# Squares folded in pairs, a root activation at a block's start, one block merged into two others, and an output stored in quarters

## The reference

```python
for l in range(2):
    sh1, sc1, g1, sh2, sc2, g2 = ada_params(c, ada_w[l], ada_b[l])       # and the same of c_ctx for ctx
    x = x + g1 * rmsnorm_2(mixer(modulate(x, norm_g[l, 0], sh1, sc1)), norm_g[l, 1])
    x = x + g2 * rmsnorm_2(swiglu(modulate(x, norm_g[l, 2], sh2, sc2)), norm_g[l, 3])
# rmsnorm_2(x, g) = x * rsqrt(mean(x * x) + 1e-6) * g;  modulate = rmsnorm_2(x, g) * (1 + scale) + shift
# the context rows go the same way in layer 0, and serve layer 1 as keys and values only
return x
```

## Time and profile before

| | us |
|---|---|
| median of 3 runs | 3593.79 (3592.45 to 3594.01) |
| the profiled execution | 3587.6 |
| its span | 3585.9 |
| PE busy | 3289.4 (92%) |
| DVE, ACT, POOL busy | 2146.1, 1456.4, 41.7 |
| granted TensorE clock, mean | 0.947 of full speed |

### The profile page before, as it was taken

One profiled execution on the slowest core, in us unless ns is written; L12 is line 12 of the kernel. 1 busy time (PEld: TensorE's weight loads), 2 busy tenths in 40 slices (PEclk: granted clock), 3 DMA queues, 4 the chain that ended last, 5 costly groups with the idle time before them and its releaser, 6 DMA issues. The chain is left out here.

```text
span 3585.9 us, 54305 instructions
## 1 busy us (share of the span) xinstructions
PE 3289.4 (92%) x20646; PEld 2841.2 (79%) x20646; DVE 2146.1 (60%) x4081; ACT 1456.4 (41%) x2274; POOL 41.7 (1%) x66
## 2 busy tenths in 40 slices
PE   6987899999999898999999999699889999979897
PEld 4844799998888677999997888488656787867797
DVE  4523489875777735699776788523673433244553
ACT  3312444444555434444444555323333332233443
POOL 0000000000000000000000000000120000000000
PEclk8988999999999999999999999799997999979999
DMA  5575576556888644676657787432453332321453
GB/s 186 157 237 191 183 219 202 173 177 186 242 242 242 197 130 153 195 206 183 176 176 222 242 242 241 133 96 65 166 193 96 102 99 88 94 61 52 123 166 123
DMA packets 225065, 596.61 MB, mean 166 GB/s; under 512 B 27424, under 2 KB 97440, under 8 KB 224576
## 3 DMA queue, kind: packets, MB, share of 16 engines
q1 hardware_dynamic: 220656, 588.17, 53.8%
q10 hardware_dynamic: 4176, 5.29, 0.5%
HBM read 558.16 MB, written 35.19 MB: 165 GB/s over the span
## 5 line engine op out<-in xcount | busy, mean ns | idle before, releaser
L2528 PE MATMUL ps<-h_split,split_layer 128*128 128x256 f32 x6144 | 773.1, 285 | 10.9 <-DVE split_layer L2317 10.9
L2528 PEld LDWEIGHTS ps<-h_split,split_layer 128*128 128x128 f32 x6144 | 746.5, 192 | 14.2 <-DVE split_layer L2317 14.2
L2674 PE MATMUL ps<-split_layer,h_split 128*128 128x512 f32 x3072 | 702.1, 391 | 13.9 <-DVE h_split L2658 13.9
L2674 PEld LDWEIGHTS ps<-split_layer,h_split 128*128 128x128 f32 x3072 | 580.4, 189 | 135.2 <-DVE split_layer L2641 14.3
L800 PE MATMUL ps<-h_parts_ffn,split_ffn 128*128 128x512 f32 (+1 forms) x2112 | 380.6, 341 | 21.2 <-DVE h_parts_ffn L273 12.0
L800 PEld LDWEIGHTS ps<-h_parts_ffn,split_ffn 128*128 128x128 f32 x2112 | 329.6, 191 | 73.7 <-issue 23.1
L2317 DVE TENSOR_TENSOR split_layer<-ring,split_layer 128x1024 fp32r<-128x1024 f32 x256 | 311.6, 1219 | 79.6 <-ACT split_layer L2456 78.0
L742 DVE TENSOR_TENSOR split_ffn<-ring,split_ffn 128x1024 fp32r<-128x1024 f32 x132 | 161.1, 1225 | 255.9 <-ACT split_ffn L724 247.1
L2641 DVE TENSOR_TENSOR split_layer<-ring,split_layer 128x1024 fp32r<-128x1024 f32 x256 | 313.7, 1225 | 0.0
L2464 ACT ACTIVATE kept_layer<-ps 128x256 f32<-128x256 f32 x256 | 98.4, 384 | 459.0 <-PE ps L2528 458.9
L2623 ACT ACTIVATE split_layer<-ring 128x1024 fp32r<-128x1024 f32 x256 | 267.5, 1045 | 4.5 <-PEq L485 4.5
(11 more groups left out here) (590 smaller groups left out, 3782.5 us busy)
## 6 DMA issues: line engine op xcount, KB each, us to landing
ring<-in_experts SPq DMA_DIRECT2D x512, 512.0 KB, 3.8
ring<-in_mod SPq DMA_DIRECT2D x96, 512.0 KB, 4.7
ring<-in_ada SPq DMA_DIRECT2D x96, 512.0 KB, 4.3
ring<-in_ffn_in SPq DMA_DIRECT2D x88, 512.0 KB, 3.6
hidden_layer<-kept_layer SPq DMA_DIRECT2D x256, 128.0 KB, 2.0
x_sb<-hidden_layer SPq DMA_DIRECT2D x256, 128.0 KB, 3.8
ring<-in_ffn_out SPq DMA_DIRECT2D x44, 512.0 KB, 3.6
ring<-in_peer_q SPq DMA_DIRECT2D x32, 512.0 KB, 3.6
```

What stands on the lines that cost most here:

```text
L2528: ins = nc.tensor.matmul(ps[:, 4 + j % 2, 0:T], w[:, part, c], self.hsplit[:, moving, k, :], start=(k == 0 and n == 0), stop=(k == KT - 1 ...
L2674: ins = nc.tensor.matmul(ps[:, 2 * t + h, :], wsplit(j, a)[:, t * P:(t + 1) * P], w[:, b, h * 512:(h + 1) * 512], start=(j == 0 and n == 0 ...
```

## The change

Five edits, the first two in `add_streamed`:

1. **Folding.** Each quarter of squares is two tiles wide. They are now added to one tile before PE sums them: POOL adds for quarters 0 and 1, DVE for quarters 2 and 3, after its last addition to x. PE then runs one tile per quarter instead of two, and waits for each fold. In the recurrent tail the hosted piece now stands after quarter 0.
2. **A root activation first.** ACT begins the block with `Sqrt` of one column into a scratch column (L971 of the new file), at all four sites.
3. **Rows in the first feed-forward tail.** SP issues `rows_load` there, PE turns the rows (bank 2) behind `widen_root`, DVE adds the bias behind its folds. They are staged in part of `selT`, another SBUF tensor.
4. **The opening block of layer 1 is gone.** The loads of `qk_g` and `axial` go to SP's list at the head of `grouped_inputs`, the rotation matrix is built by POOL there, and DVE scales it behind the entry instead of ahead of it.
5. **Output in quarters.** In the last tail SP waits for each quarter's addition and stores that quarter (256 KB), then waits for all four. `finish`'s block is gone.

```diff
@@ add_streamed @@
+            if rows or out is not None:
+                @block.sync
+                def _(sp):
+                    if rows:
+                        self.rows_load(sp, rows_name, 2, 0, 48, rows_bias)
+                    if out is not None:
+                        for i in range(QUARTERS):
+                            sp.wait_ge(summed.sem, at[summed] + i + 1)
+                            part = slice(i * per, (i + 1) * per)
+                            sp.dma_start(out[:, part, :], x[:, part, :]).then_inc(self.stored.sem, 16)
...
+                if rows:
+                    self.rows_turn(pe, 2, 0, 48, 2)
                 if counted:
-                    for k in range(KT):
-                        if k % per == 0:
-                            pe.wait_ge(self.squared.sem, at[self.squared] + k // per + 1)
+                    for i in range(QUARTERS):
+                        if i < 2:
+                            pe.wait_ge(folded.sem, at[folded] + i + 1)
+                        else:
+                            pe.wait_ge(self.vector_folded.sem, vector_folded0 + i - 1)
                         for t in range(nt):
-                            ins = mm(ps[:, 4, t:t + 1], squares[:, k, t * P:(t + 1) * P], self.ones[:, 0:1],
-                                     start=(k == 0 and t == 0), stop=(k == KT - 1), skip_group_check=True)
-                        if jobs and k == KT // 2 - 1:
+                            ins = mm(ps[:, 4, t:t + 1], squares[:, i * per, t * P:(t + 1) * P], self.ones[:, 0:1],
+                                     start=(i == 0 and t == 0), stop=(i == QUARTERS - 1), skip_group_check=True)
+                        if jobs and i == 0:
                             self.aside_products(pe, 8, 8 * len(jobs))
...
+                    for i in range(2, QUARTERS):
+                        dve.wait_ge(self.squared.sem, at[self.squared] + i + 1)
+                        v.tensor_tensor(squares[:, i * per, :], squares[:, i * per, :], squares[:, i * per + 1, :], ALU.add
+                                        ).then_inc(self.vector_folded.sem, 1)
+                if rows:
+                    self.rows_add(dve, rows_out, 2, 0, 48, 2)
...
+                @block.gpsimd
+                def _(pool):
+                    for i in range(2):
+                        pool.wait_ge(self.squared.sem, at[self.squared] + i + 1)
+                        nc.gpsimd.tensor_tensor(squares[:, i * per, :], squares[:, i * per, :], squares[:, i * per + 1, :],
+                                                ALU.add).then_inc(folded.sem, 1)
...
             def _(act):
+                nc.scalar.activation(warm, self.ones[:, 0:1], ACT.Sqrt)
@@ grouped_inputs @@
             def _(sp):
+                for dst, src in c["pairs"]:
+                    sp.dma_start(dst, src).then_inc(self.loaded.sem, 16)
                 self.stream(sp, N_M)
+            @block.gpsimd
+            def _(pool):
+                self.rotation_into(pool, c["rot"], 32)
...
                 entry.vector_begin(dve)
+                entry.vector_parts(dve, lambda: low(0))
+                dve.wait_ge(self.loaded.sem, loaded0 + 16 * len(c["pairs"]))
+                dve.wait_ge(self.pool_done.sem, self.pool_done.n)
                 v.tensor_scalar(turn_q, c["rot"], q_gain, None, ALU.mult).then_inc(turn_made.sem, 1)
-                entry.vector_parts(dve, lambda: low(0))
```

More of the change, by code:

```diff
@@ L451, in __init__ @@
         self.squared, self.summed, self.inverted = sig("squared"), sig("summed"), sig("inverted")
+        self.folded, self.vector_folded = sig("squares_folded"), sig("squares_folded_late")
         self.result_squared = sig("result_squared")
@@ L859, in linear_normed, with add_streamed @@
         return total
-    def add_streamed(self, y, parts, total, counted=True, jobs=()):
+    def add_streamed(self, y, parts, total, counted=True, jobs=(), rows=None, out=None):
         nc, v, mm, ps = self.nc, self.nc.vector, self.nc.tensor.matmul, self.ps
@@ L868, in add_streamed @@
         root, squares = self.arena.take(2, nt), self.arena.take(KT, n)
+        warm = self.arena.take(1)
+        vector_folded0 = self.vector_folded.n
         x = self.xT[:, :, c0:c1]
@@ L873, in add_streamed @@
         per = KT // QUARTERS
-        at = {s: s.n for s in (scaled, summed, counts, inverted, rooted, widened, self.squared)}
+        folded = self.folded
+        at = {s: s.n for s in (scaled, summed, counts, inverted, rooted, widened, folded, self.squared)}
+        if rows:
+            rows_name, rows_out, rows_bias = rows
+            self.stage = flat(self.selT)[:, 0:3 * P].rearrange("p (a b) -> p a b", a=3)
         if jobs:
@@ L921, in _ @@
                 if counted:
+                    for i in range(2, QUARTERS):
+                        dve.wait_ge(self.squared.sem, at[self.squared] + i + 1)
+                        v.tensor_tensor(squares[:, i * per, :], squares[:, i * per, :], squares[:, i * per + 1, :], ALU.add
+                                        ).then_inc(self.vector_folded.sem, 1)
+                if rows:
+                    self.rows_add(dve, rows_out, 2, 0, 48, 2)
+                if counted:
                     dve.wait_ge(rooted.sem, at[rooted] + 2)
                     v.reciprocal(root[:, 1, :], root[:, 1, :]).then_inc(inverted.sem, 1)
+            if counted:
+                @block.gpsimd
[4 more added lines that the diff above has]
+                                                ALU.add).then_inc(folded.sem, 1)
             @block.scalar
             def _(act):
+                nc.scalar.activation(warm, self.ones[:, 0:1], ACT.Sqrt)
                 act.wait_ge(counts.sem, at[counts] + 1)
@@ L960, in add_streamed @@
         if counted:
-            self.squared.up(QUARTERS)
+            self.squared.up(QUARTERS), folded.up(2), self.vector_folded.up(2)
         self.arena.at = mark
@@ L2984, in latent_attention, with swiglu @@
         A.at = mark
-    def swiglu(self, name, parts, gain_in, gain_out, counted, follow, hosted=()):
+    def swiglu(self, name, parts, gain_in, gain_out, counted, follow, hosted=(), rows=None, out=None):
         nc, ps = self.nc, self.ps
@@ L3048, in swiglu @@
         total = self.linear_normed(split, KT, FT, lambda part, k: hidden[:, part, k, :], y, gates, gain_out, self.arena)
-        self.add_streamed(y, gates, total, follow)
+        self.add_streamed(y, gates, total, follow, rows=rows, out=out)
         inner.close()
@@ L4225, in program @@
         core.swiglu("ffn_0", [(CTX, mods[3][1], mods[4][1], mods[5][1]), (LAT, mods[3][0], mods[4][0], mods[5][0])],
-                    gain[2], gain[3], True, True, [("ada_1", 11, 1, 2)])
+                    gain[2], gain[3], True, True, [("ada_1", 11, 1, 2)], rows=("ada_1", mod, dram["ada_b_1"]))
         if stop == 7:
@@ L4234, in program @@
         pairs = [(c["qk_g"], dram["qk_g"]), (c["axial"], dram["axial"])]
-        with core.block() as block:
-            @block.scalar
-            def _(act):
-                for dst, src in pairs:
-                    act.dma_start(dst, src).then_inc(core.loaded.sem, 16)
-                act.wait_ge(core.loaded.sem, core.loaded.n + 16 * len(pairs))
-            @block.sync
-            def _(sp):
-                core.rows_load(sp, "ada_1", 2, 0, 48, dram["ada_b_1"])
-            @block.gpsimd
-            def _(pool):
-                core.rotation_into(pool, c["rot"], 32)
-            @block.tensor
-            def _(pe):
-                core.rows_turn(pe, 2, 0, 48, 4)
-            @block.vector
-            def _(dve):
-                core.rows_add(dve, mod, 2, 0, 48, 4)
-        core.loaded.up(16 * len(pairs))
+        c["pairs"] = pairs
         gain = [norm_g[:, :, 4 + i] for i in range(4)]
@@ L4261, in program @@
         core.close_work()
-        core.swiglu("ffn_1", [(LAT, mods[3][0], mods[4][0], mods[5][0])], gain[2], gain[3], True, False)
-        finish(core, dram)
+        core.swiglu("ffn_1", [(LAT, mods[3][0], mods[4][0], mods[5][0])], gain[2], gain[3], True, False, out=dram["out"])
+        core.close_work()
 def finish(core, dram):
```

3 lines of the change are left out of this document (added).

## The result

The changed kernel took 3569.95 us, median of 4 runs (3567.95 to 3573.47), beside 3593.12 for the kernel before (4 runs, 3588.01 to 3594.01): a ratio of 0.9939, 95% interval 0.9922 to 0.9957, which is 15.5 to 28 us. The forecast was 3575.8, with 3570.0 to 3584.0 as its range; 3569.95 lies 0.05 us under its lower end. The profiled execution took 3570.68 us with a span of 3569.0, against 3587.6 and 3585.9 before: 16.9 us less.

A forecast was written before the change was run, and what follows sets the result against it. Sums of squares were taken to bound each tail that makes them, beside layer 1's opening seam and the final store. Gains 3.9 + 3.85 + 1.85 - 0.45 + 6.4 + 2.5, say 18.0 us, gave 3575.8 us, range 3570.0 to 3584.0.

The forecast's parts named there:

- recurrent tail, sums: Recurrent tail: with folds, PE's one-column sums end at 2766.3 instead of 2770.20, a gain of 3.9 us.
- first feed-forward tail, sums: First feed-forward tail: folding with POOL and DVE taking turns ends PE's sums earlier, a gain of 3.85 us.
- grouped tail, sums: Grouped tail: with folds, PE's sums end at 3347.5 instead of 3349.32, a gain of 1.85 us.
- root activation, three sites: Tails with a table load: the extra activation stands between load and root, losing 0.15 us each, 0.45 in sum.
- opening block: Start of layer 1: the 6.89 us seam becomes an ordinary 0.69 and DVE's scaling leaves the entry, gaining 6.4 us.
- output: End of the kernel: storing in quarters leaves 3.15 us after the last addition instead of 5.63, gaining 2.5 us.
- Folding and contention: Tails with squares: halved PE records, POOL and DVE additions taking whole-instruction turns; forecast 3575.8 us, chance 0.52.
- No contention: Rival for the tails: POOL and DVE don't hinder each other, gains 4.95 + 5.0 + 2.35, total 3573.0 us; chance 0.20.
- POOL last: Rival for the tails: DVE's queue keeps its turn, fold 1 comes behind it, total 3578.4 us; chance 0.12.
- Every cover named: Work moved from the opening block hides: rows beside idle PE before fold 0, two loads landing in 2 to 5 us.
- The four parts: End after the last addition: issue 0.1, store 2.4, previous quarter still moving 0.15, program end 0.5, together 3.15 us.
- the signs of being wrong: PE waiting beyond forecast times, DVE stretched over one POOL addition, layer 1's fifth weight unit late, or stages between tails moving.

The follow-up runs named there:

- u_fold: Changed kernel with only the folding undone, PE summing eight tiles and the hosted piece back behind the fourth: 3587.18 us in one profiled execution.
- u_warm: Changed kernel without the root activation at the head of the four tails: 3570.62 us in one profiled execution.
- pool_late: Changed kernel with both of POOL's folds waiting for DVE's last addition to x: 3576.1 us in one profiled execution.
- c_after: The changed kernel unaltered, run again on one chip with other variants: median of 6 runs 3568.48 us, ratio 0.9941 to the kernel before.
- u_out: Changed kernel with the output stored as before, one 1 MB DMA in a block of its own: 3569.7 us in one profiled execution.
- u_block: Changed kernel with the block that opens layer 1 restored, folds, root activation and output kept as changed: 3578.04 us in one profiled execution.
- dve_folds: Changed kernel with all four folds on DVE and POOL unused: 3571.62 us in one profiled execution.
- hosted_q2: Changed kernel with the recurrent tail's hosted piece behind quarter 2's sums instead of quarter 0's: 3580.45 us in one profiled execution.

## Where the prediction was right and where it was off, step by step

| term | predicted | measured |
|---|---|---|
| recurrent tail, sums | 3.9 (2.0 to 5.0) | 5.25; 3.57 with the low clock in both, 2.68 with the higher level in both |
| first feed-forward tail, sums | 3.85 (2.1 to 5.0) | 3.95 by u_fold; 3.87 net of the root |
| grouped tail, sums | 1.85 (0.95 to 2.35) | 1.90 by u_fold; 1.82 net |
| root activation, three sites | -0.45 | -0.3 by u_warm |
| opening block | 6.4 (5.5 to 6.9) | 6.48 to the first split; the body behind it 0.17 shorter |
| output | 2.5 (1.2 to 3.1) | 2.50 |
| sum | 18.05 | 19.46 |

The measured sum is that of the five stretches. Beside the terms it holds 0.29 us lost in the last tail and 0.06 in the seam behind the recurrent one; the body's 0.17 is not in it.

**Folding and contention.** This step decided between 3573.0, 3575.8 and 3578.4, and it went as the one stretched pair of the earlier trace rows said: whole instructions in turns. Behind the block's start I had fold 0 done at 10.83 (3173.6 - 3162.77), fold 1 by 13.23 and the sums at 18.48; the trace has 10.87, 13.14 and 18.47. The additions to x were stretched by 1.08 in sum where I had 1.3. "No contention" is out by these rows. So is "POOL last": by it fold 1 would have come behind all of DVE's work, and it was done at 13.14, ahead of the last addition's end at 14.22. (pool_late's order, with both folds behind, is worse than that rival: 21.98.)

**Recurrent tail.** The one term that left its bounds, by 0.25 us, and the reason is not in the folds. The same code up to this point has four profiles: after, c_after, u_out and u_block. PE's last 24 records, by windows of the two (us, busy of PE, PEld, DVE, ACT, POOL, granted clock, DMA share, GB/s):

after:

```profile
2765.32:2769.27 3.95, 3.39 (x28) 3.22 (x24) 0.69 (x1) 1.54 (x2) 0.00 (x0) 0.88 0.90 334
```

u_block:

```profile
2761.64:2766.92 5.28, 5.28 (x28) 5.20 (x24) 0.69 (x1) 1.54 (x2) 0.00 (x0) 0.50 0.91 327
```

At 0.50, which I had taken from the earlier trace rows as the price of all one-column sums, the tail ends at 21.28, a gain of 3.57. Another 0.30 is hidden in it: the first widening took 2.07 us in u_block and 1.77 before. At 0.88 the tail ends at 19.60. The higher level came in near the end of the hosted piece or just behind it in nine of the thirteen profiles, among them after, u_fold and dve_folds, and stayed away in before, u_block, pool_late and hosted_q2. So the term was mis-sized by a clock that I took as fixed where it varies from execution to execution. Why it came back in some and not in others is open: u_fold and u_block speak against the change as its cause. Compared like with like, the edit is worth 3.57 (before against u_block) or 2.68 (u_fold against after), both inside the bounds. The other 1.68 of the 5.25 is luck of the executions compared, and without it the five stretches would have given 17.8 us.

**Grouped tail.** Term and rows agree. So does the 0.65 us that I took for a POOL fold of 128x256: both end 0.59 us behind the DVE addition for which they wait. c_after shows 10.79 where after shows 10.29, and the whole difference is the first widening, 1.22 us against 0.71, at a granted clock of 0.50 against 1.00.

**Root activation.** Loss as argued, some 0.1 instead of 0.15.

**Opening block.** The seam kept 0.41 us, not 0.69: the split of the earlier trace rows waits for a copy of DVE's (2.17), layer 1's first split does not. Every cover named held: rows turned 3.7 us into the tail where I had some 4, and the body behind the two loads of `grouped_inputs` no longer than before (142.40 against 142.57).

**Output.** The four parts summed to 3.15; measured 3.13. The last store is issued 0.04 us behind the last addition and lands 2.6 us later, the 2.4 + 0.15 of the prediction (2.4 is the median of the four), and the span ends 0.47 us behind the landing. What I did not price is the other side of the last tail: its widening took 1.01 us at a clock of 0.63 instead of 0.71, and with the root's 0.1 it became 0.39 us longer. All but the root's share is the execution's, not the change's: in c_after it took 0.71 again, and the tail 7.50 us against 7.40 before.

**The median.** The sum is off by 1.4 us, the recurrent tail's clock for the most part. The absolute forecast is 5.85 us too high, and most of that is the base. I put the profiled execution 6.2 us below the median of three, as a fixed distance: for the profiled execution I had 3569.6, and it took 3570.68. Later runs of the kernel before spread over 22.15 us, 3578.82 to 3600.97 (11 runs on one chip), where the three I had lay within 1.6. "Runs spread by 1.6 us" was the weak sentence. The terms' own bounds reach from 3571.45 to 3582.85, so the range of 3570.0 to 3584.0 left 1.45 us below and 1.15 above for the drift of 3500 us of untouched code. That the median fell on its edge is chance; c_after's 3568.48 lies 1.5 below it. Of the signs of being wrong one did appear: the stages between the tails moved (+4.32 and -1.76), and the whole times show with what: in those 11 runs the mean granted clock was 0.940 in the longest, 0.948 and 0.949 in the two shortest. In eleven earlier ones on another chip the longest had 0.942, but the shortest 0.944 and not the highest. So part of the drift goes with the clock; what sets the clock stays open.

## What to carry to other kernels

- Price each term in its own stretch and cut both traces at the same instructions: here the grouped tail's 1.8 us and the output's 2.5 stood clear where whole times moved by 7 us on their own, and u_out would have had the wrong sign.
- Beside a busy DVE with two SBUF operands, POOL works in turns with it, one whole instruction each. Count a POOL instruction there as its own length plus the wait, and add its own length to DVE's list. Where a slower third engine hides both, as PE's sums here, it costs nothing, but four folds on DVE alone came out within 0.5 us of it in each tail. What paid was to fold early.
- Compare executions at one level of the clock before you credit a change: 1.68 of the recurrent tail's 5.25 us came from elsewhere.
- Before halving the work of a chain by folding, look whether the instruction itself is issued twice. The type of the operand halved the records here as the folds did, with nothing to wait for.

## What the runs showed of the hardware that I had not expected

- The granted clock in one and the same stretch of code was 0.50 in one execution (u_block) and 0.88 in another (after), worth 1.33 us from the first to the last of PE's last 24 records and 0.36 in the hosted piece ahead of them (3.64 us against 3.28).
- A one-column fp32 matmul is two records of 0.22 us, a two-column fp32r one is one of 0.22 us at the same clock of 0.50.
- Contention goes both ways, one whole instruction at a time: a POOL addition of 128x512 alone is 1.27 us; in the changed kernel the two in the first feed-forward tail took 2.24 and 2.23, and DVE's 128x1024 addition went from 1.22 to 2.30 for one turn. A waiting POOL came ahead of DVE's next addition, though DVE's additions stood back to back (POOL's second fold ended at 3173.28, the stretched addition 1.08 us behind it). The scalings with an operand in PSUM stayed at 1.21 beside both. The Trainium skill, "GPSIMD Engine Reference", section "Key points", names contention of GpSimd with DVE instructions that have two SBUF inputs; the trace agrees.
- A table load is placed ahead of the wait of the activation that needs it: without any warming activation it starts with the block and the root follows 0.01 us behind its end.
